# A hybrid streaming encoder step: ScalarE's root and sigmoids moved ahead of one mark's coefficients, the key row spread a tile early, an expert ring of 12 rows

## The reference, cut to what matters

```
kk = heads(k * k_k)
kk = kk / jnp.maximum(jnp.sqrt(jnp.sum(kk * kk, axis=-1, keepdims=True)), L2_EPS)
w = -jax.nn.softplus(-(w0 + jnp.tanh(xw) @ w2)) - 0.5
decay = jnp.exp(-jnp.exp(w.astype(jnp.float32)))
a = jax.nn.sigmoid(a0 + xa @ a2)
...
expert = jnp.take_along_axis(cand_i, pos, axis=-1)
gate = jax.nn.softmax(best_s, axis=-1)
u = jnp.take(down, expert, axis=0)
act = jax.nn.gelu(jnp.einsum('thed,td->the', u, t), approximate=False)
vv = jnp.take(up, expert, axis=0)
return jnp.einsum('the,thed->td', gate * act, vv)
```

## Time and profile before

| what | value |
|---|---|
| runs, lowest / median / highest | 4008.57 / 4018.62 / 4030.76 us |
| the profiled execution's own time | 3980.27 us |
| its span | 3978.5 us |
| busy: PE / DVE / ACT / POOL | 3053.6 / 2887.4 / 1419.0 / 1533.8 us |
| moved by DMA | 1424.83 MB, mean 358 GB/s |
| of it by the gathers' queue | 1223.91 MB |
| chain that ended last: DVE / PE / DMA / ACT | 31% / 28% / 13% / 7% |

### The profile page before, as it was taken

How to read it: one execution, slowest core, us unless ns; L and a number is a source line. 1 busy time by engine, 2 the same in 40 slices (tenths; PEclk the granted TensorE clock), 3 DMA queues, 4 the chain that set the end, 5 groups by cost and what they waited for, 6 DMA issues and landing times.

```text
span 3978.5 us, 43460 instructions
## 1 busy us (share of the span) xinstructions
PE 3053.6 (77%) x13880; PEld 1740.0 (44%) x13880; DVE 2887.4 (73%) x6010; ACT 1419.0 (36%) x4020; POOL 1533.8 (39%) x1323
## 2 busy tenths in 40 slices
PE   7999977778777877687778677867777778776556
PEld 4655645445453535263526353635353535352112
DVE  2221468688869886988698769976897788778775
ACT  2111133424433353335243524352435242523223
POOL 1333134333334433444244324432443244334554
PEclk9999989888898889898989898979987988888779
DMA  7234379998999999999989998999899989999998
GB/s 263 99 126 159 107 315 404 408 375 359 400 410 378 375 395 416 371 368 411 417 336 401 409 416 334 404 405 413 342 404 404 398 356 386 408 370 391 420 420 354
DMA packets 243305, 1424.83 MB, mean 358 GB/s; under 512 B 27763, under 2 KB 53107, under 8 KB 95606
## 3 DMA queue, kind: packets, MB, share of 16 engines
q0 software_dynamic: 170784, 1223.91, 76.1%
q1 hardware_dynamic: 61222, 180.44, 11.9%
q10 hardware_dynamic: 11072, 17.70, 1.3%
HBM read 1389.02 MB, written 34.17 MB: 358 GB/s over the span
## 4 chain that ended last, share of the span: by engine, by line
DVE 31%; PE 28%; DMA 13%; ACT 7%; issue 6%; POOL 1%; DVEq 0%; POOLq 0%; PEldq 0%; ACTq 0%
DVE ex_rows L1604 14%; PE mx_ps L1590 11%; DMA ex_rows<-experts,mx_expert 8%; PE mx_ps L1254 5%; DMA mx_xs<-w_q 3%; DVE mx_acc L1614 3%; DMA mx_ex<-w_out 2%; PE mx_ps L1032 2%; PE mx_ps L1039 1%; PE mx_ps L1237 1%; PE mx_ps L1035 1%; PE mx_ps L996 1%; POOL ex_rows L1549 1%; ACT ex_diag L1570 1%; DVE mx_pqb L1355 1%
## 5 line engine op out<-in xcount | busy, mean ns | idle before, releaser
L1549 POOL DMA_INDIRECT ex_rows<-experts,mx_expert x1152 | 1404.7, 1219 | 2064.3 <-PE mx_ps L1590 1241.7
L1590 PE MATMUL mx_ps<-ex_rows,ex_diag 128*128 128x512 f32 x2740 | 1481.1, 686 | 407.1 <-ACT ex_diag L1570 394.9
L1604 DVE CUSTOM_DVE_ANT_0 ex_rows<-ex_rows,mx_acc 128x1024 f32<-128x1024 f32 x1152 | 1374.2, 1222 | 209.6 <-DMA ex_rows<-experts,mx_expert 191.3
L1590 PEld LDWEIGHTS mx_ps<-ex_rows,ex_diag 128*128 128x128 f32 x2740 | 556.6, 216 | 1169.0 <-issue 1161.8
L1560 ACT ACTIVATE ex_coef<-ex_coef 128x1 f32<-128x1 f32 x1152 | 220.2, 201 | 1499.0 <-DVE ex_coef L1604 1496.5
L1614 DVE SCALAR_TENSOR_TENSOR mx_acc<-ex_rows,ex_coef,mx_acc 128x1024 f32<-128x1024 f32 x467 | 599.2, 1283 | 63.3 <-ACT ex_coef L1563 53.2
L1413 PE MATMUL mx_ps<-pj_w,pj_hT 128*128 128x432 f32 x768 | 294.0, 541 | 5.8 <-ACT mx_acc L1426 4.7
L1563 ACT ACTIVATE ex_coef<-ex_coef,mx_gate 128x1 f32<-128x1 f32 x1152 | 283.9, 284 | 10.6
L1570 ACT ACTIVATE ex_diag<-cn_ident,ex_coef 128x128 f32<-128x128 f32 x685 | 255.5, 393 | 10.7
L1413 PEld LDWEIGHTS mx_ps<-pj_w,pj_hT 128*128 128x128 f32 x768 | 147.3, 195 | 139.1 <-issue 136.4
L1560 ACT ACT_TABLE_LOAD x137 | 175.8, 1283 | 13.2 <-DVE ex_coef L1604 10.2
(11 more groups left out here) (316 smaller groups left out, 3847.6 us busy)
## 6 DMA issues: line engine op xcount, KB each, us to landing
mx_fac<-w_q SPq DMA_DIRECT2D x54, 512.0 KB, 11.9
mx_ex<-w_out SPq DMA_DIRECT2D x36, 512.0 KB, 10.3
mx_ex<-w_q SPq DMA_DIRECT2D x36, 512.0 KB, 12.0
ex_rows<-experts,mx_expert POOLq DMA_INDIRECT x1152, 11.1
mx_p_cur<-w_q SPq DMA_DIRECT2D x27, 512.0 KB, 14.0
mx_xs<-w_q SPq DMA_DIRECT2D x27, 512.0 KB, 15.5
proj_rows<-mx_acc ACTq DMA_DIRECT2D x48, 216.0 KB, 1.9
mx_fac<-w_out SPq DMA_DIRECT2D x18, 512.0 KB, 18.3
```

The source lines that it names most:

```text
L1549: pool.indirect_dma_start(rows[:, g % RING, :], None, A["experts"], bass.IndirectOffsetOnAxis(expert[:, t % 2, s:s + 1], 0))\
L1590: last = pe.matmul(bank(6 + c), diag[:, diags.due(t, n) % DIAGS, :], up[:, r, c * 512:(c + 1) * 512], start=n == 0, stop=n == len(on_pe(t) ...
L1604: dve.tensor_tensor_reduce(out=down[:, r, :], in0=down[:, r, :], in1=tn[:, :], scale=1.0, scalar=0.0, op0=ALU.mult, op1=ALU.add, accum_out ...
```

## The change

Four edits. ScalarE's `slots.upto(3)` before the root is gone, so that mark 3's coefficients are made by the next call, `upto(5)`, behind the sigmoids. The one-row matmul that spreads k_k is a function of its own, `key_gain`; for prompt tiles it is called at the end of the tile ahead, after the scores of the routing and before the remaining marks (for the first one before the loop). `G` and `H` are now parts of `pqk`, so `decays` waits for `y0_out`. The 8 KB a partition that this frees hold a twelfth ring row.

```diff
--- before.py
+++ after.py
@@ -261,7 +261,7 @@
         (0, 1, 4, 4), (1, 1, 2, 2), (2, 2, 1, 1), (4, 4, 0, 1),
         (0, 1, 8, 8), (1, 1, 4, 4), (2, 1, 2, 3), (3, 1, 2, 2), (4, 1, 1, 2), (5, 3, 1, 1), (8, 8, 0, 1)]
 NCAND = sum(n * m for _, n, _, m in CAND)
-RING = 11
+RING = 12
 DIAGS = 8
 VECTOR_CREDIT = 8
 WRING = 6
@@ -419,8 +419,6 @@
         "g2b": sb("g2b", [P, RW]),
         "keysT": sb("keysT", [P, 2, P]),
         "iota": sb("iota", [P, NCAND]),
-
-        "G": sb("G", [P, 4, PAIRS, HD]), "H": sb("H", [P, 4, PAIRS, HD]),
     }
 
 
@@ -454,8 +452,8 @@
         def flag(name, per=1, first=None):
             return Signal(ctx, nc, name, per, first)
 
-        ident, ident2, rc, bc, w2a2, g2a, g2b, keysT, iota, G, H = (C[n] for n in (
-            "ident", "ident2", "rc", "bc", "w2a2", "g2a", "g2b", "keysT", "iota", "G", "H"))
+        ident, ident2, rc, bc, w2a2, g2a, g2b, keysT, iota = (C[n] for n in (
+            "ident", "ident2", "rc", "bc", "w2a2", "g2a", "g2b", "keysT", "iota"))
 
         p_cur = sb("p_cur", [P, HEADS * P + RW])
         xs = sb("xs", [P, P_RWKV])
@@ -505,6 +503,7 @@
         kac = part(arT, 0, (RW,))
         cat = part(sa, 0, (D,))
         kk, k2, work2, work = (part(pqb, n * RW, (RW,)) for n in range(4))
+        G, H = (part(pqk, n * D, (4, PAIRS, HD)) for n in range(2))
         qT = part(pqb, 2 * RW, (PAIRS, P))
         lora = part(fac, 0, (2 * LORA + GLORA,))
         big = part(pqb, 0, (16, P))
@@ -700,7 +699,6 @@
             act.activation(loraT[:, 0:2 * P], ps[:, 0, 0:2 * P], ACT.Copy)
             act.activation(loraT[0:GLORA - P, 2 * P:3 * P], ps[0:GLORA - P, 0, 2 * P:3 * P], ACT.Copy)\
                .then_inc(loraT_ready.sem, 1)
-            slots.upto(3)
             act.wait_ge(kk_ss.sem, kk_ss.due(t, 1))
             act.activation(small[:, 1, :], small[:, 0, :], ACT.Sqrt).then_inc(kk_norm.sem, 1)
             act.wait_ge(lora_out.sem, lora_out.due(t, 1))
@@ -885,6 +883,7 @@
                                   ALU.add)\
                    .then_inc(s_ready.sem, 1)
 
+            dve.wait_ge(y0_out.sem, y0_out.due(t, 1))
             decays(0)
             for n in range(4):
                 slots.upto(18 + n)
@@ -953,13 +952,17 @@
             link.close()
 
 
+        def key_gain(pe):
+            pe.matmul(bank(4), ones(KK_ROW), g2b[KK_ROW:KK_ROW + 1, :], start=True, stop=True,
+                      tile_position=(KK_ROW, 0)).then_inc(kkc_out.sem, 1)
+
         def mix_tensor(pe, t, m, slots):
             sample, nk, width = m["sample"], m["nk"], m["width"]
             half = lambda o: slice(o * HD, (o + 1) * HD)
             if not sample:
                 pe.wait_ge(tile_end.sem, tile_end.due(t, 0))
-            pe.matmul(bank(4), ones(KK_ROW), g2b[KK_ROW:KK_ROW + 1, :], start=True, stop=True,
-                      tile_position=(KK_ROW, 0)).then_inc(kkc_out.sem, 1)
+            if sample:
+                key_gain(pe)
             slots.upto(2)
             pe.wait_ge(lora_in.sem, lora_in.due(t, 1))
             pe.transpose(ps[:, 0, 0:P], lora[:, 0:P], ident[:, :])
@@ -1716,6 +1720,8 @@
                     route_tensor(pe, t + 1, slots)
                     pe.wait_ge(sco_out.sem, sco_out.due(t + 1, 4))
                     pe.sem_inc(tile_end.sem, 1)
+                    if t + 1 < T:
+                        key_gain(pe)
                     slots.upto(MARKS)
                     ahead = experts
                 ahead.finish()
```

## The result

The changed kernel took 3990.64 us (median of 6 runs, 3983.84 to 4006.36) beside 4021.03 for the kernel before (6 runs, 4008.57 to 4030.76): a ratio of 0.9935, 95% interval [0.9911, 0.996]. The forecast was 0.987. A repeat gave 0.9948 [0.9927, 0.9969]. So the kernel is faster by 21 to 26 us, half of the 51 forecast. The profiled execution took 4006.36 us, with a span of 4004.6. That span is longer than the 3978.5 of the first profile of before.

A forecast was written before the change was run, and what follows sets the result against it. It took an almost full DMA stream and a DVE, ACT and PE chain freeing ring rows as bounds. 35 + 1 + 16 + 1 − 2.4 = 51 us off 3980.3, ratio 0.987, gave 3968 us, range 3925 to 4005.

The forecast's parts named there:

- rival A: Ring of gather rows: it buys nothing, since DMA stays full wherever DVE waits; 34 us remain, 3984 us; chance 0.20.
- The root's 35 + 1 us: Tile start: earlier root and sigmoids save 5.0 us in each of 7 tiles, 1 us in the first prompt tile.
- The ring's 16 + 1 − 2.4 us: Gather ring: twelfth row saves 16 us over 8 tiles and 1 in the last stretch; added y0 wait loses 2.4.
- rival C: Earlier root given back, at marks 7 and 8 through missing rows or in the weight phase; 4008 us; chance 0.12.
- The cap of the gain: Tile start: DVE's own path limits what the earlier root can gain to 6.4 us a tile.
- The wait, −2.4 us: DVE's decays at L868 wait 1.4 us for y0; 0.3 charged in 8 tiles, 2.4 us lost, at most 11.
- The twelfth row, 16 + 1 us: DMA dry spells: one row covers up to 7.5 us a tile, 2 taken; 16 us, plus 1 in the last stretch.
- The key row, 0: Moved one-row matmul, 1.12 us of PE, at the tile's end: counted zero, 1 us a tile to either side.
- The base: Whole run: 51 us taken off one profiled execution of 3980.3 us, then scaled by 0.987 to the 4018.62 median.
- wrong if the periods stay at 388 or more: Prompt tile periods: forecast 382 us, 385 under rival A; the prediction's own test of failure.
- Rival D: Route phase: one more gather in flight delays the w_q blocks 7.5 us a tile; 26 us slower, 4045; chance 0.06.

The follow-up runs named there:

- root alone: Kernel before with only the root and sigmoids moved ahead of mark 3's coefficients; ring of 11, G and H in own buffers, key row unmoved: 0.9957.
- fillers: Kernel before plus four 512-column matmuls that compute nothing, in PE's idle stretch ahead of y0 in the prompt tiles: 0.9909.
- fillers, root: Kernel before plus the four idle matmuls ahead of y0 and the root and sigmoids moved ahead of mark 3's coefficients: 0.9856.
- fillers, wait: Kernel before plus the four idle matmuls ahead of y0 and the decays waiting for y0; own G and H buffers, 11 rows: 0.9992.
- fillers, ring, late decays: Kernel before plus four idle matmuls, shared G and H buffers, 12 rows, and the y0 wait with the decays moved behind the first slot's dot and add: 0.9898.
- the second group: Six more idle matmuls ahead of the factors' transposes, added to the kernel before with the root moved and the four ahead of y0: 0.9816.

## Why the prediction was wrong in its size

The kernel is faster, the rows of the tile's start came as forecast, and the gain is 21 to 26 us, not 51. The forecast's 0.987 lies outside both intervals; rival A's 34 us (0.9915) lies inside that of the first result and outside that of the repeat. A was right that the ring buys next to nothing, but not for its reason, a DMA that stays full (135 GB/s in the ten microseconds above), and it was wrong, like the forecast, in the root's 36 us. That its number came close is luck.

Two terms of the sum failed. The root's 35 + 1 us took the whole shift of the tile's start for time at the end; alone it gives 17. The ring's 16 + 1 − 2.4 us gave nothing: the row is worth less than charged, and the wait more, in every tile that keeps its clock. Both were priced as if PE went on at the upper clock behind L854. Step by step, with times in tiles three to seven counted from the tile's start, its L788 (means, read from the timelines; L854 and the first L878 by their start, the last L884 by its end):

| profile | sigmoids | L854 | first map (L878) | last sum (L884) | period |
|---|---|---|---|---|---|
| before, first profile | 15.3 | 109.4 | 115.2 | 138.1 | 389.7 |
| before, second | 15.2 | 108.9 | 119.2 | 145.4 | 395.3 |
| root alone | 10.5 | 104.1 | 116.1 | 143.7 | 392.2 |
| changed kernel | 11.4 | 104.6 | 115.4 | 144.4 | 392.0 |
| fillers | 15.1 | 108.0 | 115.3 | 139.5 | 388.8 |
| fillers, root | 10.5 | 103.8 | 111.2 | 137.1 | 385.0 |
| fillers, wait | 15.2 | 108.4 | 114.0 | 145.7 | 394.8 |
| fillers, ring, late decays | 15.1 | 108.2 | 115.2 | 140.5 | 388.4 |

**The root and the sigmoids, 35 + 1 us.** A failed step, in its size. The mechanism was right: 4.7 us at the sigmoids, 4.8 at L854. But 5.0 us a tile were charged at the end, and the earlier root reaches it as 3.1 us with the clock free and 3.8 with the fillers in these tiles; the timed runs give 17 and 21 us in all. What is lost lies behind L854: the last sum comes only 1.7 us earlier with the clock free, 2.4 with the fillers. The stage of y0 and the maps gave back a part of what the tile's start had gained. That is rival C in kind, though not where C put it: with the root alone DVE waits 179.3 us for rows, in the second profile of before 175.4, so it is not in missing rows. It goes with PE's products at the lower clock: y0 is at it in 7 or 8 of 8 tiles in the five profiles without fillers that have the root moved, in 1, 4, 5 and 5 of those that don't. Why an earlier root makes the fall more frequent is not shown. (The cap of the gain, 3265.06 less 3258.6, is 6.5 us and not 6.4, which changes nothing.)

**The wait, −2.4 us.** The step whose mechanism failed. Taken as a hole of 1.4 us partly covered by L878's 1.18, it is a hole of 1.3 us as read, and costs 33 us where the clock is held at y0, since the maps behind it go on at the lower clock for longer. In tiles that are at the low clock at y0 anyway, it costs nothing; without fillers the ring's edits together come to nothing (1.0009). The upper bound of 11 us did not hold either: it counted the hole and not what PE does behind it.

**The twelfth row, 16 + 1 us.** A failed step. Measured: 7 us with an error of 8 beside the same wait, nothing beside the late decays. The rows that DVE waited for did come sooner, by some 40 us in the run; the tile got no shorter by it. The dry spells were real, but in the two looked at no slot was used for 10 us or more (GpSimd's gaps of 12.15 and 11.93 us), and a row covers 2.5 of it. The spell at the maps is not one of depth but of DVE standing still.

**The key row, 0.** It was bounded at 1 us a tile, as a matmul of 1.12 us in another place. That it also filled a gap of PE, and that the clock falls in the gap in some tiles, was not in the bound: 2.6 us in one tile of the changed kernel and 1.7 in another. The total, 22 ± 16 us in one pair and 15 ± 15 in another, both beside fillers, is not settled.

**The base.** The steps were priced in an execution that was 1% faster than the median, and the forecast scaled that away as if a uniform factor. It was not one: in tiles three to seven the difference sat in one stage, that of y0 and the maps (28.7 us from L854 to the last sum in one profile, 36.5 in the other), and this was the stage into which the wait was put and through which the root's gain had to pass. The periods that were to prove it were forecast at 382 us from one profile's 389.7; another profile of the same kernel has 395.3. They came out at 392.0 and, in the repeat, 389.9. By the sentence "wrong if the periods stay at 388 or more" it was wrong, in the size. Rival D is not seen: nothing is slower, though for the tile shown the trace of after gives no time to landing for the blocks of w_q.

## What to carry to other kernels

Read the granted clock stage by stage in two profiles of the same kernel before pricing an edit: where the two differ, any edit that moves a wait there can be worth several times its own length, in either direction. A wait of 1.3 us on DVE ahead of work that PE's small products depend on cost 4 us a tile; one slot's work put ahead of it made it free. A shorter wait for rows is not a shorter kernel: the twelfth row took some 40 us off the one, and off the other 7 with an error of 8. Where TensorE idles ahead of many small products, a few products that compute nothing may be the best change of all: here they gave 36 us and a line of order on ScalarE 21, together with the second group 0.9816.

## What the runs showed of the hardware

PE's idle time before L1047 is 3.81 or 3.82 us in every prompt tile of every profile without fillers. It was followed by y0 at the upper clock in 7 tiles of one profile of the kernel before (in one of them from the second pair on) and at 0.50 in 4 tiles of the next. With 0.38 or 0.39 us of idle time, the clock held at y0 in all 8, in every kernel with fillers. At 0.50 a pair of 64-column products took 0.63 us instead of 0.39, and the clock stayed there while PE was busy for 10 us without a gap (0.50 in 2970 to 2980). The Trainium skill, "TensorE: Matmul & The Clock Gate", section "What's actually happening", says that the count of slow matmuls at a kernel's start varies from run to run for one kernel; the traces show the like in the middle of a kernel, with 1, then 4 of 8 tiles. It puts the penalty of a ramp at under 1% of a typical span; here holding the clock at one place gave 0.9%, and what a wait there did to the clock another 0.8%.
